# One expert's weights fetched by row index, and no row sums in the first expert step: a mixture-of-experts step on one Trainium2 core

## The chip, the core and the metric

The kernel runs on one core of a Trainium2 chip. The metric is the device time of one launch in microseconds (us). Lines such as L1385 are lines of the kernel before; the changed kernel has the same statements some lines further down.

## The reference

One layer of a streaming encoder for two request groups: 256 new frames of one stream and 8 x 16 frames of running streams, 384 tokens of width 1024 in all. A mixer (three kinds of attention, gates, a projection) gives `x1`; a mixture of experts and a second layer norm give the output.

```python
def moe_ffn(x, w_router, router_bias, w_e_gate, w_e_up, w_e_down, w_s_gate, w_s_up, w_s_down):
    ...
    _, e_idx = lax.top_k(jnp.where(e_mask, sel, -jnp.inf), TOP_K)   # 8 of 64 experts for each token
    ...
    def expert_step(acc, ew):
        wg, wu, wd, g_col = ew
        hid = jax.nn.silu(t @ wg) * (t @ wu)
        return acc + g_col[:, None] * (hid @ wd), None

    routed, _ = lax.scan(expert_step, jnp.zeros_like(t), (w_e_gate, w_e_up, w_e_down, gate.T))
    shared = (jax.nn.silu(t @ w_s_gate) * (t @ w_s_up)) @ w_s_down
    return (routed + shared).reshape(b, s, d)
```

Each of the 64 experts has a gate and an up matrix of 1024 x 256 and a down matrix of 256 x 1024, float32: 1 MB each, 3 MB an expert. An expert gets 48 tokens on average. With the inputs that the reference draws, the routing gives three experts more than 64 tokens (68, 66 and 67).

## The kernel before

The program is straight-line code for five engines and their queues, which wait for each other by semaphores. Mixer, router and shared expert take the first half of the time. Then come the **expert steps**.

A step works on a pair of experts. Each has 64 slots (`CAP`), so a step has 128 rows: an indirect load on the POOL queue (`gather`, L936) fetches the tokens' rows of `x1` into `xg`, TensorE turns them, and 32 steps (`PAIRS`) cover the 64 experts. Slots without a token have an index past the end, for which the indirect load is told to leave the row out.

Experts with more than 64 tokens have the rest in further chunks of 32 slots. **Step 32**, which always runs, has four such chunks (`quad=True`), one for each of the four weight buffers `ew[0]` to `ew[3]`. Up to four chunks there is no further step. Before the change, a chunk that does not exist still has weights loaded: its entry in `table` is 0, and expert 0's 3 MB are fetched for `ew[3]`.

The steps use two sets of weight buffers by turns: `ew[0]`, `ew[1]` for the even and `ew[2]`, `ew[3]` for the odd steps. The loads are on SyncE's queue (`load_pair`, L730 to L746), for step n in the order gate, up, down, two loads of 1 MB each. The loads of gate wait until step n-2 has done its gate products, those of up for its up products, those of down for its down products. Step 32 uses both sets: its first two chunks the even buffers, its last two those that step 31 frees.

In a step, TensorE does in order (function `step`, L1377):

- gate products and up products (L1385, out into `ps_P`), waiting for the loads of each;
- turning the next step's rows (L1367, `turn`);
- turning this step's hidden values (L1392), which DVE then copies to `hidT` (L2153);
- the **row sums** of the step before (L1373, `sum_pieces`): the output rows of step n-1, `yo`, held as three bfloat16 pieces in `yo` and `rests`, are multiplied by the 0/1 matrix `back`, which puts rows at their tokens. There are six tiles of three products; DVE adds each tile to `x_sb` (L2176);
- in the first steps, `slot_tokens` (L1137), which lists the tokens of a later step;
- the down products (L1409, out into `ps_V`), which ACT scales into `yo` (L1623).

The first step has no step before it. So POOL clears `yo`, `rests` and `back[1]` ahead of it, and its row sums add zeros to `x_sb`.

While the shared expert's last products (L1355) run, `more_chunks` counts the further chunks: TensorE and DVE take turns (L1146 to L1155, L1805 to L1816), and the result is `table`, whose last number is the count. POOL's three memsets at L941 to L943 fall into the same time.

## Time and profile before

| | |
|---|---|
| three runs | 1061.83, 1063.9 and 1065.72 us, median 1063.9 |
| the profiled execution | 1063.0 us, its span 1061.2 us |
| TensorE (PE) busy | 1031.7 us, 97% |
| VectorE (DVE) busy | 596.8 us, 56% |
| ScalarE (ACT), GpSimd (POOL) busy | 182.1 us and 94.3 us |
| mean TensorE clock granted | 0.994 of full speed |
| read from HBM | 306.24 MB |

The span is the time from the first to the last instruction; what lies around it (1.8 us) is in the run's time only. PE is the matmuls, PEld the loading of their stationary side, DVE, ACT and POOL are the other engines, SP is SyncE; a q behind a name is its queue of DMA issues. The DMA share is the mean busy share of the 16 DMA engines. A load is spread over all 16 of them, and it has landed when the last of them has done its part. "Issue" is time in which an engine waited for nothing that the profile shows.

### The profile page before, as it was taken

Reading aid. Unit: us, or ns where it says so; the run is one execution under the profiler, and the core shown is the slowest. Engines: PE = TensorE matmul, PEld = TensorE weight load, DVE = VectorE, ACT = ScalarE, POOL = GpSimd, SP = SyncE. Lnnn points to the kernel's source line nnn. Section 1 sums busy time; section 2 is a strip of 40 time slices with the busy share of each in tenths; the row PEclk is TensorE's granted clock in tenths of the full one; section 3 lists DMA queues with packets and bytes.
Section 4 is the critical chain, followed back from the end, with each engine's and each line's share of the span. In section 5 each row is a group of like instructions: output and inputs, shape, how many; then the busy total and the mean of one; then the engine's idle time right before and its main releaser. Section 6 shows DMA issues by size and latency. Waiting matters only on the chain.

```text
span 1061.2 us, 17852 instructions
## 1 busy us (share of the span) xinstructions
PE 1031.7 (97%) x6592; PEld 655.5 (62%) x6625; DVE 596.8 (56%) x1477; ACT 182.1 (17%) x365; POOL 94.3 (9%) x111
## 2 busy tenths in 40 slices
PE   9999999999999999998999999999999999999985
PEld 4499579888888755466655555555555555555541
DVE  2445047787666333366785655655655655655636
ACT  1411224443323100010001101101101101101102
POOL 4140000000000000002014500000000000000000
PEclk9999999999999999999999999999999999999998
DMA  9633343533856698571599999999999999999981
GB/s 335 227 114 107 126 153 113 205 110 107 296 202 245 215 337 327 220 229 36 200 411 394 413 412 418 421 420 419 420 412 417 421 421 420 421 421 419 413 359 62
DMA packets 82332, 313.54 MB, mean 295 GB/s; under 512 B 13208, under 2 KB 24016, under 8 KB 56024
## 3 DMA queue, kind: packets, MB, share of 16 engines
q1 hardware_dynamic: 64864, 276.90, 66.2%
q10 hardware_dynamic: 10128, 19.40, 5.0%
q0 software_dynamic: 7280, 16.44, 4.4%
q8 instruction: 38, 0.62, 0.2%
q14 instruction: 22, 0.18, 0.0%
HBM read 306.24 MB, written 11.34 MB: 299 GB/s over the span
## 4 chain that ended last, share of the span: by engine, by line
PE 94%; DVE 3%; DMA 2%; issue 1%; ACT 0%; SPq 0%; DVEq 0%
PE ps_P L1385 21%; PE ps_P L1129 16%; PE ps_V L1409 11%; PE ps_V L1373 8%; PE ps_V L1321 6%; PE ps_P L1008 5%; PE ps_S L1373 4%; PE ps_V L1165 4%; PE ps_T L1367 3%; PE ps_T L1001 2%; DMA arena<-w_e_up 2%; PE ps_P L1017 1%; PE ps_P L1183 1%; PE ps_V L1355 1%; PE ps_S L1392 1%; PE ps_V L1070 1%
## 5 line engine op out<-in xcount | busy, mean ns | idle before, releaser
L1385 PE MATMUL ps_P<-arena,branch_out 128*64 128x256 f32 (+1 forms) x2176 | 233.8, 379 | 5.5 <-DMA arena<-w_e_gate 3.5
L1385 PEld LDWEIGHTS ps_P<-arena,branch_out 128*64 128x64 f32 (+1 forms) x2176 | 152.7, 135 | 94.7 <-issue 24.6
L1409 PE MATMUL ps_V<-arena,branch_out 128*64 128x512 f32 (+1 forms) x544 | 120.6, 598 | 0.0
L1623 ACT ACTIVATE weight_ring<-ps_V,merge 128x512 f32<-128x512 f32 x66 | 45.3, 687 | 379.5 <-PE ps_V L1409 379.5
L1373 PE MATMUL ps_V<-weight_ring,branch_out 128*128 128x512 bf16 x363 | 92.6, 387 | 2.1
L2149 DVE TENSOR_TENSOR branch_out<-branch_out,ps_P 128x256 f32<-128x256 f32 x33 | 13.9, 422 | 139.6 <-PE ps_P L1385 139.6
L2176 DVE TENSOR_TENSOR x_sb<-x_sb,ps_V 128x512 f32<-128x512 f32 x132 | 87.1, 682 | 0.3 <-PE ps_V L1373 0.3
L2139 DVE TENSOR_TENSOR weight_ring<-weight_ring 128x512 f32<-128x512 f32 x64 | 44.4, 693 | 68.4 <-ACT weight_ring L1623 68.4
L1129 PE MATMUL ps_P<-xT,weight_ring 128*128 128x192 f32 x432 | 79.5, 329 | 0.8 <-ACT arena L1535 0.8
L1409 PEld LDWEIGHTS ps_V<-arena,branch_out 128*64 128x64 f32 (+1 forms) x544 | 34.8, 135 | 68.7 <-issue 68.6
L1129 PEld LDWEIGHTS ps_P<-xT,weight_ring 128*128 128x128 f32 x432 | 70.2, 190 | 4.8 <-issue 4.1
L1373 PEld LDWEIGHTS ps_V<-weight_ring,branch_out 128*128 128x128 bf16 x396 | 38.3, 97 | 43.3
L1321 PE MATMUL ps_V<-branch_out,weight_ring 128*128 128x384 f32 x192 | 62.2, 487 | 0.5 <-DVE branch_out L1872 0.5
L1373 PE MATMUL ps_S<-weight_ring,branch_out 128*128 128x512 bf16 x198 | 55.4, 387 | 0.0
L1129 PE MATMUL ps_P<-x_sb,arena 128*128 128x192 f32 x288 | 53.7, 330 | 0.0
L1129 PE MATMUL ps_P<-x_sb,weight_ring 128*128 128x192 f32 x288 | 53.4, 329 | 0.0
L1321 PEld LDWEIGHTS ps_V<-branch_out,weight_ring 128*128 128x128 f32 x192 | 36.4, 190 | 25.9 <-DVE branch_out L1872 0.8
L1600 ACT ACTIVATE merge<-ps_S,small 128x256 f32<-128x256 f32 (+2 forms) x64 | 30.3, 474 | 119.1 <-DVE small L2004 119.0
L1129 PEld LDWEIGHTS ps_P<-x_sb,arena 128*128 128x128 f32 x288 | 46.9, 190 | 2.9 <-issue 2.2
L1129 PEld LDWEIGHTS ps_P<-x_sb,weight_ring 128*128 128x128 f32 x288 | 47.0, 190 | 2.2 <-issue 1.1
L2176 DVE TENSOR_TENSOR x_sb<-x_sb,ps_S 128x512 f32<-128x512 f32 x66 | 45.1, 683 | 0.0
L2117 DVE COPY branch_out<-ps_T 128x512 f32<-128x512 f32 x66 | 42.5, 686 | 4.6 <-PE ps_T L1367 0.2
(363 smaller groups left out, 1242.8 us busy)
## 6 DMA issues: line engine op xcount, KB each, us to landing
arena<-w_e_gate SPq DMA_DIRECT2D x68, 1024.0 KB, 10.5
arena<-w_e_up SPq DMA_DIRECT2D x68, 1024.0 KB, 12.4
arena<-w_e_down SPq DMA_DIRECT2D x68, 1024.0 KB, 9.5
weight_ring<-w_in SPq DMA_DIRECT2D x12, 1024.0 KB, 9.3
weight_ring<-w_in ACTq DMA_DIRECT2D x8, 1024.0 KB, 7.1
gates<-arena ACTq DMA_DIRECT2D x12, 384.0 KB, 3.2
arena<-fox_k_t SPq DMA_DIRECT2D x8, 512.0 KB, 4.1
arena<-cache_fox_v SPq DMA_DIRECT2D x8, 512.0 KB, 4.3
```

The costliest lines, as they stand in the source:

```text
L1008: last = mm(out[:, 0:w], src[:, k, j * P:(j + 1) * P], slot[:, k % 4, 0:w], start=(k == 0), stop=(k == KD - 1))
L1129: last = mm(gate_bank(i, r), w[:, k, :], x[:, k, :], start=(k == 0), stop=(k == 3))
L1165: last = mm(out[:, :], yT[:, k, j * P:(j + 1) * P], slot[:, k % 4, :], start=(k == 0), stop=(k == KD - 1))
L1321: last = mm(out[:, 0:T], slot[:, k, m * P:(m + 1) * P], oT[:, br, k, :], start=(k == 0), stop=(k == 3))
L1367: last = nc.tensor.transpose(ps["T"][half][:, k * P:(k + 1) * P], xv[:, half * 4 + k, :], ident)
L1373: last = mm(out[:, :], rows[:, (k // 2) * P:(k // 2 + 1) * P], upper[c][:, (k % 2) * 512:(k % 2 + 1) * 512], start=(c == 0), stop=(c == 2))
L1385: last = mm(bank[r:r + wide, 0:256], xgT[q][:, k, r:r + wide], w[h][:, k, :], start=(k == 0), stop=(k == KD - 1))
L1409: last = mm(ps["V"][half][r:r + wide, :], hidT[:, m, r:r + wide], ew_down[h][:, m, half * 512:(half + 1) * 512], start=(m == 0), stop=(m = ...
L1623: fn(yo[:, half * 512:(half + 1) * 512], ps["V"][half][:, :], ACT.Copy, scale=now_info[:, q, 1:2])\
L2117: V.tensor_copy(xgT[par][:, half * 4:half * 4 + 4, :], ps["T"][half][:, :].rearrange("p (k c) -> p k c", k=4)).then_inc(xgT_ready, 1)
L2139: V.tensor_tensor(rests[:, 0, cs], yo[:, cs], upper[0][:, cs], ALU.subtract).then_inc(rest_ready, 1)
L2176: return V.tensor_tensor(xv, xv, tiles[k % 3][:, :], ALU.add)
```

## The change

It has two parts.

**The fourth chunk.** SyncE loads three chunks' weights for step 32. The fourth's are loaded by three indirect loads on the POOL queue, 128 rows of 8 KB each (2048 numbers for every partition), by an index in `idx[:, 2:3]`. That is expert x 128 + partition, and 8192 more where there are fewer than four chunks, which is past the end of the matrix: then all rows are left out. `more_chunks` gets two DVE operations more for the inputs, one more product on TensorE, and three DVE operations for the index. TensorE waits for the fourth's loads in step 32 by semaphores of their own.

**The first step.** It has no row sums and no adds of them. The semaphores are raised at the start instead, and POOL's clearing of `back[1]`, `yo` and `rests` is gone.

```diff
@@ more_chunks, TensorE
-                    mm(ps["S"][1][0:1, P + MORE:P + MORE + 1], cc("ones")[0:E, 0:1], chunks[0:E, :], start=True, stop=True).then_inc(chunks_done, 1)
+                    mm(ps["S"][1][0:1, P + MORE:P + MORE + 1], cc("ones")[0:E, 0:1], chunks[0:E, :], start=True, stop=True)
+                    mm(ps["S"][1][:, 256:258], cc("ones")[0:E, 0:P], fourth[0:E, :], start=True, stop=True).then_inc(chunks_done, 1)
@@ more_chunks, VectorE
-                    V.scalar_tensor_tensor(is_in[0:E], since[0:E], chunks[0:E], begun[0:E], ALU.is_lt, ALU.mult).then_inc(begun_ready, 1)
+                    link(V.scalar_tensor_tensor(is_in[0:E], since[0:E], chunks[0:E], begun[0:E], ALU.is_lt, ALU.mult))
+                    V.tensor_copy(fourth[0:E, 1:2], chunks[0:E])
+                    V.tensor_tensor(fourth[0:E, 0:1], is_in[0:E, 3:4], cc("tok", E)[:, 0:1], ALU.mult).then_inc(begun_ready, 1)
                 else:
                     V.tensor_copy(table[0:1, 0:MORE + 1], ps["S"][1][0:1, P:P + MORE + 1]).then_inc(flag_ready, 1)
+                    V.tensor_scalar(fourth_row[:, 0:1], ps["S"][1][:, 256:257], float(P), cc("tok")[:, 0:1], ALU.mult, ALU.add)
+                    link(V.tensor_scalar(fourth_row[:, 1:2], ps["S"][1][:, 257:258], 3.5, float(E * P), ALU.is_lt, ALU.mult))
+                    V.tensor_scalar(idx[:, 2:3], fourth_row[:, 0:1], fourth_row[:, 1:2], None, ALU.add).then_inc(fourth_ready, 1)
@@ load_chunks, SyncE
-                    load_pair(PAIRS + 1, 1, e[2:4])
+                    load_pair(PAIRS + 1, 1, e[2:3])
@@ POOL
-            nc.gpsimd.memset(back[1], 0.0).then_inc(back_ready, 1)
...
-            nc.gpsimd.memset(yo, 0.0).then_inc(pieces_ready, 1)
-            nc.gpsimd.memset(rests, 0.0).then_inc(pieces_ready, 1)
             nc.gpsimd.memset(xg[1], 0.0).then_inc(xg_cleared, 1)
...
+            def load_fourth(to, matrix, signal):
+                pool.indirect_dma_start(to, None, matrix, bass.IndirectOffsetOnAxis(ap=idx[:, 2:3], axis=0),
+                                        bounds_check=E * P - 1, oob_is_err=False).then_inc(signal, 16)
+            pool.wait_ge(fourth_ready, 1)
+            pool.wait_ge(gate_done, PAIRS)
+            load_fourth(ew[3][:, 0:2048], a["w_e_gate"][0].rearrange("e (p k) f -> (e p) (k f)", p=P), fourth_loaded["gate"])
+            pool.wait_ge(up_done, PAIRS)
+            load_fourth(ew[3][:, 2048:4096], a["w_e_up"][0].rearrange("e (p k) f -> (e p) (k f)", p=P), fourth_loaded["up"])
+            pool.wait_ge(down_done, 2 * PAIRS)
+            load_fourth(ew[3][:, 4096:6144], a["w_e_down"][0].rearrange("e (p m) n -> (e p) (m n)", p=P), fourth_loaded["down"])
@@ step, TensorE
+                    if fourth:
+                        pe.wait_ge(fourth_loaded[m], 16)
...
-                pe.wait_ge(pieces_ready, 2 * n + 2)
-                pe.wait_ge(back_ready, n + 1)
-                for k in range(6):
-                    if k >= 2:
-                        pe.wait_ge(added, 6 * n + 4 + k)
-                    sum_pieces(tiles[k % 3], back[1 - q], k).then_inc(summed, 1)
+                if sums:
+                    pe.wait_ge(pieces_ready, 2 * n + 2)
...
+                else:
+                    pe.sem_inc(summed, 6)
                 pe.wait_ge(hidT_ready, n + 1)
...
+                if fourth:
+                    pe.wait_ge(fourth_loaded["down"], 16)
@@ VectorE, before the first step
-            dve.sem_inc(added, 6)
+            dve.sem_inc(added, 12)
+            dve.sem_inc(back_ready, 1)
+            dve.sem_inc(pieces_ready, 2)
...
-            pair(0, 0)
+            pair(0, 0, sums=False)
```

On TensorE, the first expert step stands so in the kernel before, from the turning of the hidden values to the next step's gate products:

```order
L1392 MATMUL ps_S<-cst,branch_out 128x128 x2
L1373 MATMUL ps_V<-weight_ring,branch_out 128x512 x6
L1373 MATMUL ps_S<-weight_ring,branch_out 128x512 x3
L1373 MATMUL ps_V<-weight_ring,branch_out 128x512 x6
L1373 MATMUL ps_S<-weight_ring,branch_out 128x512 x3
L1137 MATMUL ps_S<-merge,branch_out 128x6 x3
L1409 MATMUL ps_V<-arena,branch_out 64x512 x8
```

And so in the changed kernel (L1409, L1151 and L1431 there are L1392, L1137 and L1409 here):

```order
L1409 MATMUL ps_S<-cst,branch_out 128x128 x2
L1151 MATMUL ps_S<-merge,branch_out 128x6 x3
L1431 MATMUL ps_V<-arena,branch_out 64x512 x8
L1402 MATMUL ps_P<-arena,branch_out 64x256 x32
L1382 MATMUL ps_T<-cst,small 128x128 x8
```

Eighteen products of 128x512 are gone from between the turning and `slot_tokens`. All the other steps keep theirs.

On POOL, the memsets ahead of the first steps stand so before (`weight_ring` holds `yo`, `rests` and `xg[1]`, in this order), between two gathers:

```order
L925 MEMSET small 128x1024
L926 MEMSET branch_out 128x384
L936 DMA small<-x_rows,idx 128x1024
L941 MEMSET weight_ring 128x1024
L942 MEMSET weight_ring 128x2048
L943 MEMSET weight_ring 128x1024
L936 DMA weight_ring<-x_rows,idx 128x1024
```

And so in the changed kernel:

```order
L929 MEMSET small 128x1024
L939 DMA small<-x_rows,idx 128x1024
L944 MEMSET weight_ring 128x1024
L939 DMA weight_ring<-x_rows,idx 128x1024
L939 DMA small<-x_rows,idx 128x1024
```

One memset is left where three were, so the gather behind it comes up sooner.

At the end of POOL's program the changed kernel has three loads more, behind the last gathers and ahead of the test for further chunks:

```order
L939 DMA weight_ring<-x_rows,idx 128x1024
L939 DMA small<-x_rows,idx 128x1024
L976 DMA arena<-w_e_gate,idx 128x2048
L976 DMA arena<-w_e_up,idx 128x2048
L976 DMA arena<-w_e_down,idx 128x2048
L673 TENSOR_LOAD table
```

Nothing is queued behind them on POOL that runs when there are up to four chunks.

## Rows read from the trace of the kernel before

**Rows 1.** Windows: us in the window, each engine's busy us, clock, DMA share, GB/s
```profile
core 0: us, PE busy (x) PEld busy (x) DVE busy (x) ACT busy (x) POOL busy (x), PEclk, DMA share, GB/s
522.46:538.90 16.44, 16.38 (x115) 9.34 (x114) 14.54 (x33) 1.76 (x3) 0.99 (x1) 1.00 0.90 359
...
600.00:1000.00 400.00, 398.34 (x2697) 215.28 (x2722) 228.85 (x439) 43.98 (x75) 29.54 (x31) 1.00 1.01 418
```

**Rows 2.** The chain that ended last, steps 30 and 31: start, us, what
```profile
990.80 6.91 PE ps_P L1385 x64
...
1006.69 6.93 PE ps_P L1385 x64
```

**Rows 3.** Timeline of PE, step 31's down products and step 32's gate, up
```profile
1018.92 3.65 PE L1409 MATMUL ps_V<-arena,branch_out 128*64 128x512 f32 x16
...
1026.09 3.66 PE L1385 MATMUL ps_P<-arena,branch_out 128*32 128x256 f32 x64 [3.52 <-DMA arena<-w_e_gate]
...
1031.04 3.66 PE L1385 MATMUL ps_P<-arena,branch_out 128*32 128x256 f32 x64 [1.28 <-DMA arena<-w_e_up]
```

**Rows 4.** By line: last gate and up loads, then the third step's up loads
```profile
L738 SPq DMA_DIRECT2D arena<-w_e_gate x2: 333/334/336, 1010.3 to 1010.8; - x2
DMA to landing us min/median/max: 9.2/12.2/15.1
...
L742 SPq DMA_DIRECT2D arena<-w_e_up x2: 333/358/382, 1013.6 to 1014.1; - x2
...
DMA to landing us min/median/max: 10.9/13.8/16.8
...
L742 SPq DMA_DIRECT2D arena<-w_e_up x2: 333/497/661, 517.8 to 518.3; - x2
...
DMA to landing us min/median/max: 8.6/10.0/11.4
```

**Rows 5.** Timeline of SyncE's queue, the third step's down loads
```profile
527.38 0.81 SPq L746 DMA_DIRECT2D arena<-w_e_down  x2
```

**Rows 6.** The chain that ended last, the first expert step
```profile
519.19 1.29 PE ps_V L1373 x5
520.48 0.68 PE ps_S L1373 x3
521.15 1.35 PE ps_V L1373 x6
522.51 0.68 PE ps_S L1373 x3
523.19 0.57 PE ps_S L1137 x6
523.75 3.58 PE ps_V L1409 x16
```

**Rows 7.** Timeline of DVE in the first expert step: the copy to `hidT`
```profile
519.68 0.41 DVE L2153 COPY branch_out<-ps_S 128x256 f32<-128x256 f32 x1
```

**Rows 8.** Timeline of the chunk count beside POOL's memsets
```profile
495.79 1.80 POOL L942 MEMSET weight_ring<- 128x2048 f32 x1
...
496.05 1.56 DVE L1806 TENSOR_SCALAR merge<-cst,merge 64x10 f32<-64x10 f32 x1
...
497.53 0.97 POOL L943 MEMSET weight_ring<- 128x1024 f32 x1
...
497.83 0.71 DVE L1808 TENSOR_SCALAR merge<-cst,merge 64x64 f32<-64x64 f32 x1
...
498.60 0.27 PE L1150 MATMUL ps_S<-merge,cst 64*64 64x1 f32 x2 [1.16 <-DVE merge L1808]
```

**Rows 9.** The gathers by tile, 560 to 1000 us; then queue 0, 900 to 947.6
```profile
L936 POOL DMA_INDIRECT weight_ring<-x_rows,idx x14: 988/988/1060, 566.9 to 973.5; - x14
...
DMA to landing us min/median/max: 7.2/8.4/9.6
...
q0 software_dynamic: 431, 1.27, 6.8%
```

More of the change, by code:

```diff
@@ L510, in build @@
         empty = N.take(1)
+        fourth = N.take(2)
+        fourth_row = N.take(2)
         XO = Space(R_O, o_cols)
@@ L604, in build @@
         flag_ready = sem("flag_ready")
+        fourth_ready = sem("fourth_ready")
+        fourth_loaded = {m: sem(f"fourth_{m}") for m in ("gate", "up", "down")}
         hidden_ready = sem("hidden_ready")
@@ L1375, in sum_pieces, with step @@
                 return last
-            def step(n, q, loaded, quad=False, turned=None, listed=False, lists=LISTED):
+            def step(n, q, loaded, quad=False, turned=None, listed=False, lists=LISTED, sums=True, fourth=False):
                 pe.wait_ge(xgT_ready, 2 * n + 2)
-                for sems, w, bank, finished in ((gate_loaded, ew_gate, ps["P"][0], gate_done), (up_loaded2, ew_up, ps["P"][1], up_done)):
+                for sems, w, bank, finished, m in ((gate_loaded, ew_gate, ps["P"][0], gate_done, "gate"), (up_loaded2, ew_up, ps["P"][1], up_done, "up")):
                     for c, at in loaded:
                         pe.wait_ge(sems[c], at)
+                    if fourth:
+                        pe.wait_ge(fourth_loaded[m], 16)
                     for k in range(KD):
@@ L1393, in step @@
                 last.then_inc(hid_turned, 1)
-                pe.wait_ge(pieces_ready, 2 * n + 2)
-                pe.wait_ge(back_ready, n + 1)
-                for k in range(6):
-                    if k >= 2:
-                        pe.wait_ge(added, 6 * n + 4 + k)
-                    sum_pieces(tiles[k % 3], back[1 - q], k).then_inc(summed, 1)
+                if sums:
+                    pe.wait_ge(pieces_ready, 2 * n + 2)
+                    pe.wait_ge(back_ready, n + 1)
+                    for k in range(6):
+                        if k >= 2:
+                            pe.wait_ge(added, 6 * n + 4 + k)
+                        sum_pieces(tiles[k % 3], back[1 - q], k).then_inc(summed, 1)
+                else:
+                    pe.sem_inc(summed, 6)
                 pe.wait_ge(hidT_ready, n + 1)
@@ L1419, in _ @@
             for n in range(LISTED - 3):
-                step(n, n % 2, [(n % 2, 32 * (n // 2 + 1))], turned=(n + 1) // 2 + 1, listed=True, lists=n + 3)
+                step(n, n % 2, [(n % 2, 32 * (n // 2 + 1))], turned=(n + 1) // 2 + 1, listed=True, lists=n + 3, sums=n > 0)
             with pe.Fori(3, EARLY) as i:
@@ L1426, in _ @@
             chunks_n = chunk_count(pe)
-            step(PAIRS, 0, [(0, 32 * (PAIRS // 2 + 1)), (1, 32 * (PAIRS // 2 + 1))], quad=True)
+            step(PAIRS, 0, [(0, 32 * (PAIRS // 2 + 1)), (1, 32 * (PAIRS // 2) + 16)], quad=True, fourth=True)
             def last_sums(n, split):
@@ L2143, in split_rows, with pair @@
                     V.tensor_tensor(rests[:, 1, cs], rests[:, 0, cs], upper[1][:, cs], ALU.subtract).then_inc(pieces_ready, 1)
-            def pair(n, q, turned=True, listed=True, split=True):
+            def pair(n, q, turned=True, listed=True, split=True, sums=True):
                 dve.wait_ge(silu_ready, n + 1)
@@ L2153, in pair @@
                 V.tensor_copy(hidT.rearrange("p m c -> p (m c)"), ps["S"][0][:, 0:256]).then_inc(hidT_ready, 1)
-                for k in range(6):
-                    dve.wait_ge(summed, 6 * n + k + 1)
-                    add_tile(k).then_inc(added, 1)
+                if sums:
+                    for k in range(6):
+                        dve.wait_ge(summed, 6 * n + k + 1)
+                        add_tile(k).then_inc(added, 1)
                 V.tensor_copy(now_info[:, q, :], info[:, bass.ds(n, 1), :].rearrange("p o c -> p (o c)")).then_inc(now_copied, 1)
```

2 lines of the change are left out of this document (1 added, 1 removed).

## The prediction

> **What bounds the kernel now.** I read the windows first, to see which engine is never idle. In the expert steps two things are: TensorE is busy for 398.34 of 400 us at full clock, and the DMA engines' share is 1.01 [rows 1]. So it has to be told which of the two holds the other. The chain gives TensorE's pace: a step takes 1006.69 - 990.80 = 15.89 us, all of it products [rows 2]. For the DMA side I read landings. A load has landed when the slowest of 16 engines has done its part; I follow that one and call it the slowest ring. The third step's up loads: the second is issued at 518.3 and the longest landing is 11.4, so it lands at 529.7. The last up loads: 1014.1 + 16.8 = 1030.9 [rows 4]. Between lie 31 pairs in 501.2 us, 16.17 us a pair. The slowest ring is 0.28 us a step slower than TensorE, and falls behind step by step. In the middle nobody sees that, since loads are issued two steps ahead. At the end it shows: step 32 takes its last two chunks from buffers that step 31 has just freed, so their loads are issued only at 1010.3 and 1013.6 [rows 4]. TensorE comes free at 1018.92 + 3.65 = 1022.57, waits 3.52 us for the gate loads, and after its gate products 1.28 us for the up loads [rows 3]. The end of the kernel is thus set by the slowest ring, and 4.8 us of waiting are open there.
>
> One thing more must be known: whether that ring ever waits for an issue. The third step's up loads land on it at 529.7, and the next loads, down, are issued at 527.38 [rows 5], 2.3 us before. Landings get longer from there on, so the ring has work from 514.5 us to the end. Other rings do run dry at that place: the window there has a DMA share of 0.90 [rows 1], 0.10 x 16.44 = 1.6 us of idle time on average.
>
> **The change, part by part.**
>
> *No row sums in the first step.* The 18 products take 1.29 + 0.68 + 1.35 + 0.68 = 4.00 us of TensorE [rows 6]. They covered the copy to `hidT`, which ends at 519.68 + 0.41 = 520.09 [rows 7]. `slot_tokens` waits for it, and started at 523.19; it can now start at about 520.15. So TensorE gets 3.04 us, not 4.00. DVE's six adds were under these products and go with them.
>
> *The memsets on POOL.* DVE's L1806, on 64 x 10 numbers, takes 1.56 us and ends at 497.61; the memset of `rests` runs from 495.79 to 497.59 [rows 8]. L1808 beside the next memset takes 0.71. TensorE waits 1.16 us for it before L1150 [rows 8]. I read this as DVE held up by POOL. The Trainium skill, page "SBUF — State Buffer", section "Who interferes with whom", says that a DVE `tensor_scalar` of such a kind and a GpSimd instruction share a port pair, and that the second fully blocks until the first is done. By that rule the trace agrees, to 0.02 us. In the change one memset of 0.97 us is left [rows 8]; it takes the place of the first of three, whose time ended at 495.79, and so is over before L1806. So L1806 and L1808 shrink to what neighbours of that size take, TensorE has its shared-expert products to do meanwhile, and the whole 1.16 us go. Against it stands one product more in `more_chunks`, and DVE's additions: L1150's 0.27 us is the nearest row for the product [rows 8], I take 0.2; the two DVE operations before it lie under 2 us of shared-expert products, and the three behind it feed nobody on this path. Net 0.95 us. Bounds: nothing gained, if the gather that moves into this place holds DVE as well (then 0.3 lost), and 1.16. This gain is unlike the first: it comes *before* the first expert step, so the loads that wait for that step's gate products are issued 0.95 us sooner, and the slowest ring moves with it.
>
> *Three loads fewer, 3 MB.* The last gate loads land on the slowest ring at 1010.8 + 15.1 = 1025.9, the up loads at 1030.9 [rows 4]: two loads in 5.0 us, 2.5 us each. One gate load fewer takes 2.5 us off the wait for gate, and one gate and one up load fewer take 5.0 us off the wait for up. With gate in at 1025.9 - 2.5 = 1023.4 and 3.7 us of gate products, up would be wanted at 1027.1 and is there at 1025.9: the 1.28 us are gone too.
>
> *Three indirect loads of nothing.* POOL spends 0.99 us on a gather, which lands after 7.2 to 9.6 us under full DMA load [rows 9]. That a row left out costs nothing is seen in queue 0: three gathers in 47.6 us moved 1.27 MB, 310 rows of 4 KB and not 384 [rows 9]. Gate's is issued when step 31's gate products are done, some 16 us before step 32 begins, up's 3.5 us later; both are there before their weights. Down's is issued at about TensorE's arrival, lands by 10.6 us later at the most, and is wanted 12 us after gate starts (4 + 4 of products, 4 of row sums). So all three are free. Cover gone, each us of lateness would cost a us.
>
> *What becomes of the 3.04 us.* TensorE reaches step 32 3.04 + 0.95 = 4.0 us sooner, at 1018.6. But the slowest ring was never idle, so its gate load is there no sooner for it. TensorE then waits longer. Only what that ring idled at 527 to 530 us can be won back. The bounds are 0 (it lands 2.3 us after the issue) and the 1.6 us average of all; I take 0.3, since the ring that ends last is the one with the least idle time. The skill's page "DMA: Bandwidth & Descriptors", section "Latency and other measured facts", says that two of the 16 engines are usually slower than the others; if it is they from start to end, this term is 0. No view here tells the engines apart.
>
> **The sum.** Gate starts at 1025.9 + 0.15 - 2.5 - 0.95 - 0.3 = 1022.3 against 1026.09, 3.75 us sooner; the wait of 1.28 goes: 5.0 us. From the up products on all is as before. 1063.0 (the profiled execution) - 5.0 = 1058.0. That execution is 0.9 below the median of the three runs, which gives 1058.9 from there; I say 1058.5.
>
> **Rivals.**
>
> *TensorE sets the end (0.15).* If the rings that end last are ones that ran dry early, or the issues that come sooner let DMA work denser, step 32 starts with TensorE's arrival: 4.0 + 3.52 + 1.28 = 8.8 us, 1054.7. For it: the 1.6 us of idle time. Against it: it needs 3.7 us from the slowest ring, more than any idle time seen.
>
> *The left-out rows are not free, or not left out (0.10).* The three loads would take the slowest ring as long as SyncE's did, 2.5 us each, and only 0.95 + 0.3 stay: 1061.8 to 1062.6, no measurable change. Against it: the 1.27 MB [rows 9].
>
> *DVE is held as before, and part of the ring's gain is lost (0.10).* POOL's descriptor work for the gather stands where the memset stood. Without the 0.95, or with a ring that has a slower share elsewhere, 3 to 4 us are left: 1059.5 to 1061.
>
> *An indirect load is late: the other side (0.05).* Down's load is issued by POOL at about 1018.6 + 1.0. Before, the down products began at 1039.8 (1031.04 + 3.7, then 0.5 for the hidden values and 4 of sums). If it landed more than 20 us after its issue, the kernel would be slower; at 25 us 1043.6 + what follows, 1066.8. For it: landings grow with the queue ahead. Against it: no gather took over 9.6 [rows 9].
>
> The rest, 0.60, is my forecast, whose own range is 1056.5 to 1060.5.
>
> **How the numbers follow.** This kernel's runs differ by 0.4%, so 0.3%, 3.2 us, is about what can be told. Faster by more than that: my forecast (nearly all of it, 0.58), TensorE at the end (0.15) and half of the third rival (0.05), 0.78. No change: 0.10 + 0.05 + 0.02 = 0.17. Slower 0.05. The range reaches from the second bound (1054.7) to what remains with only the loads gone and a high draw of the runs, 1061.5; it leaves out the late load and most of the rows that are not free.
>
> **What the next profile would show.** L1806's successor at 0.2 us instead of 1.56, and no wait before L1150's; the first step's down products about 4.0 us sooner; steps of 15.9 us with no wait; at step 32 one wait of some 4 us for gate, although it starts sooner, and none for up; the last gate load landing near 1022. HBM reads 3.1 MB lower. The prediction is wrong if step 32 begins without a wait (the ring was not the bound), or if its wait names a load of the fourth chunk.

## The result: 1056.8 us, 0.6% faster, and the profile after

The changed kernel takes 1056.77 us (median of 11 runs, 1054.76 to 1060.52), the kernel before 1063.13 in the same comparison (11 runs). The ratio is 0.9938, 95% interval 0.9926 to 0.9950, so 5.3 to 7.9 us faster. The profiled execution of the changed kernel took 1056.77 us, with a span of 1054.7 against 1061.2 before. Lines have moved by 14 to 27: L1385 is now L1402, L1409 L1431, L1150 L1164, L1806 and L1808 L1828 and L1830, L2153 L2180.

Timeline around the chunk count of the changed kernel, on POOL, DVE and TensorE (it answers to [rows 8]; columns: start us, busy us):
```profile
494.87 0.96 POOL L944 MEMSET weight_ring<- 128x1024 f32 x1 [4.79 <-PE ps_P L1198]
...
496.73 1.03 POOL L939 DMA_INDIRECT weight_ring<-x_rows,idx  x1 [0.90 <-POOL weight_ring L944]
...
496.02 0.22 DVE L1828 TENSOR_SCALAR merge<-cst,merge 64x10 f32<-64x10 f32 x1
...
496.47 0.25 DVE L1830 TENSOR_SCALAR merge<-cst,merge 64x64 f32<-64x64 f32 x1
...
497.35 0.27 PE L1164 MATMUL ps_S<-merge,cst 64*64 64x1 f32 x2
...
500.11 0.38 PE L1170 MATMUL ps_S<-merge,cst 64*128 64x2 f32 x2
```
The small operation that took 1.56 us takes 0.22, the next 0.25 in place of 0.71, and TensorE no longer waits ahead of its L1164. L1170 is the added product. The first expert step starts at 509.87, 0.80 sooner than before (510.67). These are two single executions. The experiments below have seven more profiles of kernels whose program is the same up to this point, and in those eight the first step starts anywhere from 508.79 to 509.99; so the 0.80 is known to about half a us. Inside the two traces it is 1.16 of a wait less, 0.45 of work more (from the start of L1164, before L1150, to the first step: 12.52 in place of 12.07), and 0.09 from ahead of the count.

The first step without row sums (timeline of DVE, then TensorE; it answers to [rows 6, 7]), and then the last down products of step 31 and step 32's gate and up products (it answers to [rows 3]):
```profile
518.88 0.41 DVE L2180 COPY branch_out<-ps_S 128x256 f32<-128x256 f32 x1
...
519.35 0.83 PE L1151 MATMUL ps_S<-merge,branch_out 128*128 128x6 f32 x6 [1.03 <-DVE branch_out L2180]
520.11 3.65 PE L1431 MATMUL ps_V<-arena,branch_out 128*64 128x512 f32 x16
...
1015.43 3.65 PE L1431 MATMUL ps_V<-arena,branch_out 128*64 128x512 f32 x16
...
1021.13 7.11 PE L1402 MATMUL ps_P<-arena,branch_out 128*32 128x256 f32 x128 [2.04 <-DMA arena<-w_e_gate]
```
The first down products start 3.6 us sooner; 1.03 us of a wait that the row sums had covered is in the open. At step 32 one wait is left, 2.04 us for gate. Gate's and up's products now stand in one row of 128, so there is none between them. They end at 1028.24, before at 1031.04 + 3.66 = 1034.70: 6.46 us sooner, the whole difference of the spans (6.5).

The last loads (DMA view of 1006 to 1021 us: KB, us from issue to landing; then windows, with the columns of [rows 1], which they answer to):
```profile
arena<-w_e_gate SPq DMA_DIRECT2D x1, 1024.0 KB, 14.0
arena<-w_e_up SPq DMA_DIRECT2D x1, 1024.0 KB, 13.3
...
arena<-w_e_gate,idx POOLq DMA_INDIRECT x1, 7.4
arena<-w_e_up,idx POOLq DMA_INDIRECT x1, 8.1
arena<-w_e_down,idx POOLq DMA_INDIRECT x1, 6.4
```
```profile
518.90:535.35 16.45, 15.94 (x111) 9.15 (x113) 13.54 (x32) 1.76 (x3) 0.99 (x1) 1.00 1.00 400
600.00:1000.00 400.00, 398.37 (x2692) 214.35 (x2717) 228.97 (x438) 43.99 (x75) 27.56 (x29) 1.00 1.01 418
```
In the middle of the kernel TensorE's busy time is the same to 0.03 us and the DMA share the same. At the start of the expert stage the DMA share has gone from 0.90 to 1.00. The indirect loads land in 6.4 to 8.1 us, long before anyone needs them: the last, down's, is issued at 1019.89, and the down products start at 1033.35.

### The profile page after: what moved, and what is told of

It is laid out like the page before. It is cut to its first block, busy times and chain, and to the rows that moved or that the text cites. A ratio compares the mean times of both kernels' runs of the same rounds, so it can differ in the third digit from the quotient of the medians.

```text
span 1054.7 us, 17820 instructions
## 1 busy us (share of the span) xinstructions
PE 1028.1 (97%) x6577; PEld 654.1 (62%) x6609; DVE 592.6 (56%) x1476; ACT 182.2 (17%) x365; POOL 94.3 (9%) x111
## 3 DMA queue, kind: packets, MB, share of 16 engines
q1 hardware_dynamic: 64432, 273.75, 66.0%
HBM read 306.24 MB, written 11.34 MB: 301 GB/s over the span
## 4 chain that ended last, share of the span: by engine, by line
PE 94%; DVE 3%; DMA 1%; issue 1%; ACT 0%; DVEq 0%; SPq 0%
PE ps_P L1402 21%; PE ps_P L1143 16%; PE ps_V L1431 11%; PE ps_V L1388 8%; PE ps_V L1336 6%; PE ps_P L1022 5%; PE ps_S L1388 4%; PE ps_V L1180 4%; PE ps_T L1382 3%; PE ps_T L1015 2%; DMA arena<-w_e_gate 1%; PE ps_P L1031 1%; PE ps_V L1370 1%; PE ps_P L1198 1%; PE ps_V L1084 1%
## 5 line engine op out<-in xcount | busy, mean ns | idle before, releaser
L1402 PE MATMUL ps_P<-arena,branch_out 128*64 128x256 f32 (+1 forms) x2176 | 233.6, 379 | 2.9 <-DMA arena<-w_e_gate 2.0
L1402 PEld LDWEIGHTS ps_P<-arena,branch_out 128*64 128x64 f32 (+1 forms) x2176 | 152.8, 135 | 91.7 <-issue 21.5
L1431 PE MATMUL ps_V<-arena,branch_out 128*64 128x512 f32 (+1 forms) x544 | 120.6, 598 | 0.0
L1388 PE MATMUL ps_V<-weight_ring,branch_out 128*128 128x512 bf16 x352 | 89.8, 387 | 2.0
L2204 DVE TENSOR_TENSOR x_sb<-x_sb,ps_V 128x512 f32<-128x512 f32 x128 | 84.5, 682 | 0.3 <-PE ps_V L1388 0.3
L1431 PEld LDWEIGHTS ps_V<-arena,branch_out 128*64 128x64 f32 (+1 forms) x544 | 34.8, 135 | 68.7 <-issue 68.6
```

The lines of the kernel that those rows point to most:

```text
L1388: last = mm(out[:, :], rows[:, (k // 2) * P:(k // 2 + 1) * P], upper[c][:, (k % 2) * 512:(k % 2 + 1) * 512], start=(c == 0), stop=(c == 2))
L1402: last = mm(bank[r:r + wide, 0:256], xgT[q][:, k, r:r + wide], w[h][:, k, :], start=(k == 0), stop=(k == KD - 1))
L1431: last = mm(ps["V"][half][r:r + wide, :], hidT[:, m, r:r + wide], ew_down[h][:, m, half * 512:(half + 1) * 512], start=(m == 0), stop=(m = ...
L2204: return V.tensor_tensor(xv, xv, tiles[k % 3][:, :], ALU.add)
```

## Experiments

The sections below use one number worked out in the same way for every profile: from the start of the first expert step (its first gate product) to the landing of the last gate load. It is taken as the time that the slowest ring needs for the expert stage. That holds as long as TensorE doesn't hold the last issues back; where it is late by a long wait in step 6, the number grows with it. Before: 1025.9 - 2.5 (the load that the change drops) - 510.67 = 512.7 us. After: 1006.84 + 14.0 - 509.87 = 511.0 us. So 1.7 of the 6.4 us were won by the rings inside the stage. The table has it beside the waits of TensorE (view of waits, 490 to 1060 us). The twelve have 5 to 12 runs each, in three batches on three chips, each batch beside the kernel before on the same chip (medians 1063.3, 1063.4 and 1062.7). So the ratios are what compares kernels of different batches.

| run | median us | ratio to before, 95% interval | first step starts | wait for a gather, step 6 | wait for gate, step 32 | ring time |
|---|---|---|---|---|---|---|
| before | 1063.1 | | 510.67 | 0 | 3.5 (+1.3 up) | 512.7 |
| changed | 1056.8 | 0.9938 (0.9926 to 0.9950) | 509.87 | 0.1 | 2.0 | 511.0 |
| e1_step_only | 1060.1 | 0.9976 (0.9961 to 0.9990) | 509.50 | 1.9 | 2.4 | 510.9 |
| e2_fourth_only | 1060.8 | 0.9977 (0.9965 to 0.9988) | 511.67 | 2.9 | 0 | 514.4 |
| e3_reorder | 1056.3 | 0.9941 (0.9923 to 0.9960) | 508.79 | 2.1 | 0 | other order |
| e4_late_down | 1057.1 | 0.9938 (0.9922 to 0.9954) | 508.90 | 0.1 | 1.5 | 510.6 |
| e5_memsets_back | 1058.6 | 0.9952 (0.9939 to 0.9966) | 513.99 | 3.4 | 0 | 515.0 |
| e6_no_fourth | 1055.2 | 0.9923 (0.9909 to 0.9937) | 509.43 | 2.2 | 0 | 511.0 |
| e7_reorder_gather7 | 1053.8 | 0.9913 (0.9900 to 0.9927) | 509.05 | 0 | 0 | other order |
| e8_fourth_gather7 | 1059.5 | 0.9964 (0.9950 to 0.9977) | 511.12 | 0 | 1.5 | 513.2 |
| e9_late_downs | 1058.9 | 0.9963 (0.9951 to 0.9976) | 509.99 | 1.6 | 2.7 | 513.3 |
| e10_gather7 | 1056.8 | 0.9940 (0.9918 to 0.9961) | 509.39 | 0 | 2.6 | 511.5 |
| e11_fourth_moves | 1063.8 | 1.0009 (0.9993 to 1.0024) | 509.26 | 4.0 | 4.9 | 519.4, one load more |
| e12_memsets_again | 1059.5 | 0.9971 (0.9956 to 0.9987) | 511.51 | 1.7 | 0.4 | 511.0 |

### The two halves of the change

e1_step_only is the kernel before with the first step's part: no row sums, no clears of `yo` and `rests`. Its edit is the changed kernel with the fourth chunk's loads on SyncE again:
```diff
-                    load_pair(PAIRS + 1, 1, e[2:3])
+                    load_pair(PAIRS + 1, 1, e[2:4])
```
and without `load_fourth`, its index and its waits.

> The kernel before with the second part of the change alone: no row sums in the first step, the memsets of yo, rests and back[1] gone; SyncE loads all four chunks. My theory (the slowest DMA ring sets when step 32 begins): TensorE reaches step 32 about 3.5 us sooner than before, but its gate products start only 2.6 us sooner (the 0.8 us by which the first step starts sooner, and 1.8 us that the ring wins), the wait for gate grows from 3.5 to about 4.4 us and the one for up stays at 1.2: 2.6 us faster than before, 0.25%. If TensorE set the end, 3.5 us or more and waits as before. If the ring won only the 0.3 us of my prediction: 1.2 us.

Measured: 1060.09, 2.5 us below before by the ratio (1.1 to 4.1). That is what the changed kernel's profile gives for this half: 0.8 for the start and 1.7 to 1.8 for the rings. The time came as expected, the waits did not: 4.4 us for gate and 1.2 for up were expected, and there are 2.4 for gate and none for up. The other 2 us of gate's wait stand in step 6. In place of up's, the gate and up products themselves took 8.80 us where they take 7.11, at half the clock for a while (last section). The view of waits (what waited, what ended it: us in total, times, longest) shows something that the kernel before doesn't have:
```profile
PE ps_P L1389 <- DMA arena<-w_e_gate: 2.4, 1, 2.4
PE ps_T L1369 <- DMA weight_ring<-x_rows,idx: 1.9, 1, 1.9
```
L1369 is `turn`: the transposes of the next chunk's rows, which GpSimd gathers. This is in step 6, chunk 7's rows.

e2_fourth_only is the kernel before with the other half: the changed kernel with the lines below, and with the clear of `back[1]`, the adds and the semaphores as they were
```diff
+            nc.gpsimd.memset(yo, 0.0).then_inc(pieces_ready, 1)
+            nc.gpsimd.memset(rests, 0.0).then_inc(pieces_ready, 1)
...
-                step(n, n % 2, [(n % 2, 32 * (n // 2 + 1))], turned=(n + 1) // 2 + 1, listed=True, lists=n + 3, sums=n > 0)
+                step(n, n % 2, [(n % 2, 32 * (n // 2 + 1))], turned=(n + 1) // 2 + 1, listed=True, lists=n + 3)
```

> The kernel before with the first part of the change alone: the fourth chunk's weights by three indirect loads, row sums and memsets as before. My theory: the last gate load lands one load (2.5 us) sooner on the slowest ring, so TensorE waits 1.0 us for gate in place of 3.5 and not at all for up: 3.8 us faster, 0.36%. If the two parts were independent of each other, e1 and e2 would sum to the change's 6.4 us. If the left-out rows cost the ring time: under 1 us faster.

Measured: 1060.79, 2.4 us below before (1.3 to 3.7), short of the 3.8 us that the two terms for the missing loads add up to. In its profile step 32 waits for no weights, where 1.0 us for gate was expected. The first step starts 1.0 late, and step 6 waits 2.9 us for the same gather:
```profile
PE ps_T L1385 <- DMA weight_ring<-x_rows,idx: 2.9, 1, 2.9
```
So a second wait, which one profile of the kernel before doesn't show, holds TensorE ahead of the one that was argued over. Each half alone gives about 2.5 us, the two together 6.6.

### Is it the order of the last loads?

e3_reorder: SyncE issues the last pairs' gate and up loads ahead of their down loads (`load_pair` is told which of its loads to issue).
```diff
-                    load_pair(PAIRS, 0, e[0:2])
-                    load_pair(PAIRS + 1, 1, e[2:3])
+                    load_pair(PAIRS, 0, e[0:2], "gu")
+                    load_pair(PAIRS + 1, 1, e[2:3], "gu")
+                    load_pair(PAIRS, 0, e[0:2], "d")
+                    load_pair(PAIRS + 1, 1, e[2:3], "d")
```

> The changed kernel, with SyncE's last loads in another order: gate and up of both chunk pairs of step 32 first, then the down loads of both. No work less, only the two down loads of the first pair no longer lie ahead of the last gate load. My theory: the last gate load lands 5.0 us sooner on the slowest ring, TensorE's 2.04 us of waiting at step 32 are gone, and the time is 2.0 us below the changed kernel's, 8.4 us (0.8%) below the kernel before. If the wait came from the late issue and not from the queue on the ring (issue to landing), the wait stays. If the down loads come too late in their new place, the down products wait.

Measured: 1056.27, no difference to the changed kernel that can be told where 2.0 us were expected, though the wait for gate is gone. In its place, in step 6:
```profile
613.91 1.16 PE L1384 MATMUL ps_T<-cst,weight_ring 128*128 128x128 f32 x8 [2.05 <-DMA weight_ring<-x_rows,idx]
```
POOL's timeline of this run shows who is late. The gather is issued last in a chain of eight rounds of row scatters, each of which waits for the landing of the round before, and of three loads of the table:
```profile
595.98 0.97 POOL L959 DMA_INDIRECT slot_rows<-merge,row_idx  x1 [3.15 <-DMA slot_rows<-merge,row_idx]
...
602.33 0.60 POOL L967 DMA_DIRECT2D weight_ring<-slot_rows  x1 [2.82 <-DMA slot_rows<-merge,row_idx]
...
605.33 1.06 POOL L941 DMA_INDIRECT weight_ring<-x_rows,idx  x1 [0.32 <-issue]
```
Chunk 7's gather has its list of rows and its free buffer long before: the wait is one of order alone. That can be tested without taking a wait away.

e7_reorder_gather7 is e3 with
```diff
+                if k == 6:
+                    gather(7, 1)
...
-            gather(7, 1)
             gather(8, 0)
```

> The changed kernel with the last pairs' gate and up loads issued ahead of their down loads (as in the run with that order before), and GpSimd's gather of the eighth chunk's rows issued after the seventh of the eight rounds of row scatters instead of behind all of them. If the 2.1 us that TensorE waited for that gather is why the reordering alone gave 0.5 us, the wait is gone, TensorE reaches the last step about 2 us sooner and finds its weights there: 1054.3 us. Rival: the time is bound by the DMA rings, which land the down loads no sooner; then TensorE waits for the down load in their place and the time stays at 1056.3.

Measured: 1053.79 (1053.35 to 1054.51), 9.2 us below before by the ratio and about 3 below the changed kernel (2.7 by the ratios, whose intervals touch at their ends): the fastest version. Its view of waits has no DMA wait left in the expert stage; the rest is the same as in the changed kernel:
```profile
PE ps_S L1154 <- DVE branch_out L2183: 1.0, 1, 1.0
PE ps_P L1405 <- DVE branch_out L2147: 0.9, 1, 0.9
PE ps_S L1412 <- DVE branch_out L2179: 0.6, 1, 0.6
PE ps_V L1373 <- DVE branch_out L2142: 0.2, 1, 0.2
```

e10_gather7 has the gather's move alone.

> The changed kernel with the gather of the eighth chunk's rows issued after the seventh round of row scatters, and nothing else. By the theory that two waits overlap (a gather in step 6 that holds TensorE by 0.1 to 2.2 us, and the last gate load, which the rings bring no sooner), taking the first away alone only lengthens the second, which is then 2 to 3 us: 1056.3 to 1056.8, while both edits together gave 3.0 us. Rival: the gather is worth 2 us by itself: 1055.

Measured: 1056.84, as the first theory has it, with
```profile
PE ps_P L1403 <- DMA arena<-w_e_gate: 2.6, 1, 2.6
```
Each of the two edits alone gives nothing that can be told (0.5 and 0 by the medians), both together 3.0. A wait in step 6 and a wait in step 32 stand in line: TensorE that comes sooner past the first waits longer at the second.

e8_fourth_gather7 is e2 with the gather's move.

> The kernel before with the fourth chunk's part alone (the run of that name before) and the gather of the eighth chunk's rows issued earlier as in the run beside this one. That part alone gave 2.5 us of 3.8 expected, with 2.9 us of waiting for this gather in its profile. If the missing 1.3 us went there, the wait is gone and the time is 1059.4 to 1059.8 (3.5 to 3.9 below before). Rival: the part is worth only 2.5 us; then 1060.8 stays. With row sums in the first step, the last gate load should land about 512.7 us after the first expert step starts; 511 would mean that the 1.8 us by which the changed kernel's rings came out ahead is not the row sums' doing.

Measured: 1059.49, 3.8 us below before by the ratio (2.4 to 5.3). The missing 1.3 us of e2 are there by the medians, though the intervals of the two runs overlap. With row sums the ring time is 513.2; e10, which differs by the first step's part alone, has 511.5.

### Where the rings won 1.7 us

e4_late_down: pair 2's down loads wait for the gate products of the next step, and so are issued about as late as before, against step 0's start.
```diff
+                if late:
+                    sp.wait_ge(gate_done, n)
```

> The changed kernel, in which the third step's two down loads are issued some 3.4 us later, when the second step's gate products are done, so at about the time after the stage's first issue at which the kernel before issued them. Nothing else is changed. If the slow ring stood idle there in the kernel before, and the change's gain of 1.8 us more than I had worked out comes from closing that gap, the last gate load lands about 1.8 us later than in the changed kernel, the wait grows from 2.0 to 3.8 us and the time by 1.8 us. If the gain came from anything else, no difference from the changed kernel.

Measured: 1057.08, no slower than the changed kernel, and a ring time of 510.6. The late issue did open a hole again (window at 524.9), and still the rings ended no later. But it is not the hole of the kernel before. There GpSimd's gather of chunk 3's rows falls into it too, issued at 526.41, 15.7 us after the first step's start; in e4 that gather is out at 520.93, 12.0 us after. Over the six us that begin 14.0 us after the first step's start, the DMA share is 0.70 before, 0.99 in the changed kernel and 0.81 in e4. Windows of before, of 4 us each, taken further down the stage, have a second one:
```profile
526.67:530.67 4.00, 4.00 (x38) 2.49 (x36) 3.00 (x6) 0.69 (x1) 0.73 (x1) 1.00 0.64 206
558.67:562.67 4.00, 4.00 (x33) 2.16 (x31) 2.82 (x7) 1.28 (x2) 0.97 (x1) 1.00 0.87 294
```
The same two places of the changed kernel, then of e4:
```profile
525.87:529.87 4.00, 4.00 (x42) 2.63 (x40) 3.86 (x6) 0.39 (x1) 0.00 (x0) 1.00 1.00 348
557.87:561.87 4.00, 4.00 (x40) 2.65 (x38) 1.46 (x3) 0.39 (x1) 1.58 (x2) 1.00 1.00 386
```
```profile
524.90:528.90 4.00, 4.00 (x42) 2.63 (x40) 3.86 (x6) 0.39 (x1) 0.00 (x0) 1.00 0.73 231
556.90:560.90 4.00, 4.00 (x40) 2.66 (x38) 1.46 (x3) 0.38 (x1) 2.35 (x2) 1.00 1.01 418
```
Before, some rings run dry a second time, in step 3, at a share of 0.87. After and in e4 they don't.

The share is a mean over the rings. The slowest is seen in the landings of the third step's down loads, before, then in the changed kernel, then in e4:
```profile
L746 SPq DMA_DIRECT2D arena<-w_e_down x2: 332/355/378, 527.4 to 527.8; - x2
...
DMA to landing us min/median/max: 7.3/8.9/10.4
```
```profile
L750 SPq DMA_DIRECT2D arena<-w_e_down x2: 333/356/379, 523.8 to 524.2; - x2
...
DMA to landing us min/median/max: 8.3/9.8/11.3
```
```profile
L752 SPq DMA_DIRECT2D arena<-w_e_down x2: 328/380/433, 526.3 to 526.7; - x2
...
DMA to landing us min/median/max: 6.3/7.4/8.5
```
Before, the second lands at 527.8 + 10.4 = 538.2, 8.5 us after the second up load (529.7 [rows 4]). The next two loads, the fourth step's gate, take 5.0 us from landing to landing. So on the ring that lands last, too, some 3.5 us went to something other than these loads: to the gather's packets, or to nothing. In the changed kernel the same distance is 535.5 - 529.8 = 5.7. Counted from the first step's start, the down loads land at 27.5 us before, 25.6 in the changed kernel and 26.3 in e4. The loads and gathers issued up to there are the same in the three. So the kernel before is 1.9 us behind here already, and e4 brings back only 0.7 of that. For the sixth step's gate loads, which are issued in step 3, it is 65.8, 63.5 and 63.5.

e9_late_downs delays the down loads of pairs 2 to 5 in e4's way.

> The changed kernel with the down loads of pairs 2 to 5 each issued about 3.4 us later, behind the next pair's gate products (an earlier run did so for pair 2 alone and its last gate load still landed 510.5 us after the first step's start). If the 1.8 us by which the rings come out ahead without the row sums are won because these loads are issued 3.6 us sooner, the last gate load lands 512 to 513 us after the first step's start, and TensorE waits for it (or the wait for the row gather in step 6 takes up to 2 us of that). If they are won otherwise, it lands at 510.5 to 511.0. The time: 1057.5 to 1058.5 by the first, 1056.8 by the second.

Measured: 1058.91 and a ring time of 513.3, so 2.3 us later than in the changed kernel, as the first theory has it (0.3 and 0.4 above the ends of what it gave). The holes are back, with one at 542 that the kernel before doesn't have:
```profile
525.99:529.99 4.00, 4.00 (x42) 2.63 (x40) 3.86 (x6) 0.39 (x1) 0.00 (x0) 1.00 0.63 205
541.99:545.99 4.00, 4.00 (x40) 2.64 (x38) 3.53 (x8) 0.39 (x1) 0.00 (x0) 1.00 0.94 328
557.99:561.99 4.00, 4.00 (x40) 2.66 (x38) 1.47 (x3) 0.39 (x1) 0.97 (x1) 1.00 0.85 290
```
In e9 the down loads of pair 2 land as in e4, 26.3 us after the first step's start, but the sixth step's gate loads only at 66.0.

Over the table: with row sums in step 0 the ring time is 512.7, 513.2 and 514.4 (the last one with 2.9 us of waiting in step 6), without them 510.6 to 511.5 in six profiles (e4's with one pair's late loads among them), without them and with four pairs' late loads 513.3. The seventh profile without them is e5's, with 515.0: there TensorE waits 3.4 us in step 6, runs slower for some us after it, and issues the last loads late. So down loads that are issued late in the first steps do cost the rings: 2.3 us in e9, and 1.7 where the row sums delay them. Which of the two holes cost the kernel before its 1.7 isn't shown: its landings are behind from the first one on, e9 loses most at the second.

### The clears on GpSimd

e5_memsets_back puts the two clears back, beside VectorE's chunk count.
```diff
+            nc.gpsimd.memset(yo, 0.0).then_inc(pieces_ready, 1)
+            nc.gpsimd.memset(rests, 0.0).then_inc(pieces_ready, 1)
             nc.gpsimd.memset(xg[1], 0.0).then_inc(xg_cleared, 1)
...
-            dve.sem_inc(pieces_ready, 2)
```

> The changed kernel with GpSimd's two clears of yo and the rests buffer put back where they stood, beside VectorE's counting of chunks; everything else as changed. If the clears slow VectorE's small operations there, the operation at the first of the two small copies takes 1.6 us again in place of 0.22, the first expert step starts 0.8 us later after TensorE's last idle ahead of it, and the time is 0.8 us above the changed kernel's (1057.6 beside 1056.8). Rival: the short operation comes from something else in the change (the extra product, the smaller set of columns); then it stays at 0.2 us and the time at 1056.8.

Measured: 1058.62, where 1057.6 was expected; its profiled execution took 1065.0, far above the other five (1057.0 to 1059.1), so the same kernel was run once more as e12_memsets_again.

> The kernel with GpSimd's two clears put back, once more, since the profiled execution of the earlier run had TensorE's granted clock at 0.72 over the last products ahead of the first expert step, and its time stands 1.9 us above the changed kernel's where 0.8 was expected. If the clears cost only VectorE's short operations, this run gives 1057.2 to 1058.0 and a profile whose first step starts at 510.5 to 511. Rival: TensorE's longer idle there costs more in some executions; then the time is again 1058.5.

Measured: 1059.53 over 12 runs (1057.2 to 1064.0), above both of the expected numbers; the interval of its ratio doesn't touch the changed kernel's. Timeline of e12 at the chunk count, on DVE, POOL and TensorE:
```profile
496.09 2.46 DVE L1830 TENSOR_SCALAR merge<-cst,merge 64x10 f32<-64x10 f32 x1
...
495.83 1.81 POOL L945 MEMSET weight_ring<- 128x2048 f32 x1
497.58 0.96 POOL L946 MEMSET weight_ring<- 128x1024 f32 x1
...
499.08 0.27 PE L1166 MATMUL ps_S<-merge,cst 64*64 64x1 f32 x2 [1.59 <-DVE merge L1832]
```
The operation on 64 x 10 numbers ends at 498.55, with the 498.54 of the clear of `xg[1]`: it was held over that clear and the one of `rests`, where before it ended with the clear of `rests`, and the next operation was held over the one of `xg[1]` [rows 8]. TensorE so waits 1.59 us where the changed kernel doesn't wait, and the first step starts 1.6 us later (511.51 against 509.87), not 0.8. In time it is 1.9 and 2.8 us in the two runs by the medians, 1.5 and 3.5 by the ratios; what makes the rest isn't shown.

### The loads that move nothing

e6_no_fourth has no fourth loads and no waits for them.
```diff
-                    if fourth:
-                        pe.wait_ge(fourth_loaded[m], 16)
```

> The changed kernel without the three indirect loads of the fourth chunk and without TensorE's three waits for them. The inputs need no fourth chunk, so nothing that is added up is left out. If indirect loads whose every row is left out are free, the time is that of the changed kernel (1056.8 within 0.4) and TensorE waits about 2 us for the last gate load as there. Rival: their packets take their turn on the DMA rings; then it is 0.3 to 1 us faster. For the size of what the missing row sums give back to the DMA rings: without row sums the last gate load should land about 511 us after the first expert step starts, as in the three earlier runs without them (510.5 to 511.0), where the two with them gave, one load fewer counted, 512.7 and 514.4.

Measured: 1055.24, 1.5 us below the changed kernel's median; the two intervals overlap. Its ring time is 511.0 as there. The 2 us of waiting that were expected for gate stand in step 6 (2.2) instead. In the changed kernel the packets of the first two of these loads take little (DMA view, queue 0 from 1006 to 1021 us: packets, MB, share of 16 engines):
```profile
q0 software_dynamic: 288, 0.00, 1.1%
```
That is 144 packets to a load, and 1.1% of 15 us = 0.16 us of the rings for both. So by the profiles they are free to 0.2 us; by the times it can't be excluded that they cost some 1.5.

e11_fourth_moves makes the loads real: the bound that tells whether there is a fourth chunk is lowered, so that 3 MB are moved for a chunk without rows.
```diff
-...257:258], 3.5, float(E * P)
+...257:258], 2.5, float(E * P)
```

> The changed kernel with the bound at which a fourth chunk is taken to be there lowered from 3.5 to 2.5 chunks, so that GpSimd's three indirect loads move their 3 MB (weights of an expert for a chunk that has no rows) as they would with inputs that need it. One load more ahead of the last step costs 2.5 us at the rings' rate: the wait for the gate weights grows from 2.0 to 4.5 us or a little more, and one for up or down weights may stand behind it: 1059.3 to 1060.6. Rival: written by GpSimd's queue in rows of 8 KB they come slower than SyncE's loads: 1062 or more, above the kernel before's 1060 with its row sums alone gone.

Measured: 1063.83, 7.1 us above the changed kernel and as slow as before: the second expectation's number, but not its reason. The chain at step 32 (start, us) and the DMA view have, in the profiled execution (1066.65, one of the slower of the twelve):
```profile
1011.82 16.87 DMA arena<-w_e_gate
1028.68 0.24 issue
1028.92 9.21 PE ps_P L1402 x128
```
```profile
arena<-w_e_gate,idx POOLq DMA_INDIRECT x1, 11.1
```
GpSimd's load is issued at 1012.5 and there by 1023.6, five us ahead of SyncE's own last gate load, which comes 2.9 us later than in the changed kernel after its issue. The wait for gate is 4.9 us, as expected. The rest of this profile's loss is a 4.0 us wait in step 6, ahead of which nothing differs from the changed kernel, and TensorE's clock, below. So a gate load that moves its 1 MB costs the rings 2.9 us here, near the 2.5 us of SyncE's. That all of the 7.1 us come from the 3 MB isn't shown.

## Why the prediction was right, and where it was off

**The bound: right.** The DMA rings set the start of step 32, and TensorE only its arrival. Steps stay at 15.9 us, and the one wait left in the changed kernel is for gate. The rival in which TensorE sets the end needed 8.8 us; 6.4 came. With both DMA waits taken away (e7) it is 9.2 against before: the time that this rival forecast is reached only when the loads are reordered too.

**Three loads fewer, 2.5 + 1.28 us: right.** e8 has this term by itself, without the wait in step 6: 3.8 us (2.4 to 5.3). The wait for up is gone in every run without the load.

**The clears, 0.95 us: right in kind, 0.80 between the two kernels**, known to about half a us. The wait of 1.16 us is gone whole; the added product and what goes with it took 0.45 in place of 0.2. e5 and e12 put the clears back and the short operation is long again. The Trainium skill's rule on the shared port pair (page "SBUF — State Buffer", section "Who interferes with whom") says that whichever of the two issues first keeps the pair for its whole instruction, and the other is blocked. Before, the trace agrees to 0.02 us; in e12 it was held over two in a row and ended 0.01 us after the second, which the rule as it stands doesn't say. The third rival, in which the gather takes the clear's place and holds DVE, was hardly tested here: the gather is issued at 496.73, when L1830 has just ended (496.72). But in e12 a `TENSOR_SCALAR` on 64 x 92 numbers starts at 499.94, inside the gather's issue (499.43 to 500.46), and takes 0.26 us, as it does in the changed kernel where no gather stands beside it.

**The indirect loads, 0: right by the profile**, to 0.2 us. They land in 6.4 to 8.1 us; no wait names them in any run.

**What becomes of the 3.04 us: this step was mis-sized, 0.3 taken and 1.7 measured.** The prediction says "the slowest ring was never idle" and "Only what that ring idled at 527 to 530 us can be won back". The mechanism (the ring keeps what it idled, TensorE waits off the rest) is right. The size is not, and with it the reading that the next loads, issued 2.3 us before the last one lands, left that ring nothing to lose. The landings on the same trace are 8.5 us apart there, where 5.0 is the rate; part of the 3.5 us is the gather, but counted from the first step's start these loads land 1.9 us later than in the changed kernel, which had the same loads and gathers to carry. Windows further down have a second hole, at 558.67 to 562.67, that the prediction didn't look for. e9 shows that late early loads cost 1.7 us and more; e4, with a smaller first hole alone, loses nothing. Whether the ring that ends last stood idle in these holes or was slower for another reason isn't shown, nor how the 1.7 us fall to the two. That the mean idle time of the first window, 1.6 us, lay near the 1.7 is chance: e4's hole has some 1.1 us of mean idle time (6 x 0.19) and costs nothing. By the Trainium skill's statement that two of the engines are usually slower (page "DMA: Bandwidth & Descriptors", section "Latency and other measured facts") the prediction had a case in which this term is 0. It measured 1.7. No view here tells the engines apart.

**The wait for gate: 2.0 and not 4.** Its products start at 1021.13 where 1022.3 was forecast, since the rings were 1.4 us better and the start 0.15 worse. And TensorE comes free at 1015.43 + 3.65 = 1019.08 where 1018.6 was forecast.

**The sum.** 0.8 + 2.5 + 1.3 + 1.7 = 6.3 against 6.46 measured in the profiles and 5.0 predicted; the range held. Of the signs, the wait for gate came at half its size, and the first step's down products 3.6 us sooner in place of 4.0.

**The forecast's check on HBM was badly chosen.** The line stands at 306.24 MB in the page before, in the page after and in e11's, though e11 moved 3 MB more than the changed kernel. The moved bytes show elsewhere, in queue 1: 273.75 MB after, 276.90 before.

**What was not in the prediction at all** is the gather in step 6. The one profile of before has no wait there; in eleven profiles without the gather's move it is 0 to 4.0 us. It goes with how much of half a change shows (e1, e2, e3); the changed kernel's profile has 0.1 us of it, and e10 shows that taking it away from the whole change gives nothing as long as the wait for gate stands behind it.

## What to carry to other kernels

That a load is issued before the one ahead of it has landed doesn't show that its ring lost nothing. Compare how far apart successive loads land (8.5 us here, where 5.0 is the rate), and look for holes in short windows over the whole stage, not at the first gap alone. An experiment that is to bring a hole back has to bring back everything that fell into it, small gathers too. Two waits in line on one engine hide each other: take both away before judging either, and look into several executions, since a wait at the end of a chain of dependent small DMAs was 0 in one and 4 us in another. When GpSimd clears memory beside VectorE's short operations, the price depends on which of them stands at the gap between two clears.

## What the runs showed that had not been expected

TensorE's granted clock fell to half in some executions behind a wait. Windows of e11: the first stretch is the wait for gate of 4.9 us, the next two the products behind it; then the clock is back.
```profile
1024.00:1028.00 4.00, 0.07 (x2) 0.00 (x0) 1.96 (x3) 0.69 (x1) 0.99 (x1) 0.79 0.92 317
1028.00:1030.00 2.00, 1.07 (x12) 0.68 (x16) 0.00 (x0) 0.00 (x0) 0.00 (x0) 0.50 0.96 373
1030.00:1032.00 2.00, 2.00 (x25) 1.01 (x20) 0.00 (x0) 0.00 (x0) 0.00 (x0) 0.50 0.98 414
...
1034.00:1036.00 2.00, 2.00 (x44) 1.23 (x40) 0.00 (x0) 0.38 (x1) 0.00 (x0) 1.00 0.17 66
```
0.50 is 1.2 GHz in place of 2.4. The block of gate and up products took 9.2 us, in the changed kernel 7.11. The same happened behind the 2.7 us wait of e9 (0.57 and 0.58 over 4 us, block 8.8 us), the 2.4 us wait of e1 (block 8.80) and the 3.4 and 4.0 us waits for the gather in e5 and e11. It did not happen behind waits of 2.0 (changed kernel), 2.6 (e10), 2.9 (e2) and 3.5 us (before), where the clock stands at 1.00. So the length of the wait alone doesn't decide it. What does is open. Where it happened at step 32, the block of products took 1.7 to 2.1 us longer. This may make part of the spread between executions, and of what e7 won; neither is shown.

In e5's profile the clock was 0.72 over 500 to 512 us, and the last products ahead of the first step took 9.52 us where they take 7.13 in the other profiles. e12, the same kernel with the same wait of 1.6 us ahead of them, had 1.00 there.
